# One stage instead of five between attention and the feed-forward network of a two-block layer kernel

## The reference

```
proj = rmsnorm(x, norm1_g) @ w_in           # x_rnn, g_rnn, q/k/v twice, f_logit, gates
x_rnn = causal_dwconv(x_rnn, 4 taps)
r, i  = sigmoid(x_rnn by blocks @ w_r + b_r), sigmoid(x_rnn by blocks @ w_i + b_i)
a     = exp(-8 * r * softplus(-a_param))
h_t   = a_t * h_(t-1) + sqrt(1 - a_t^2) * (i * x_rnn)_t      # the recurrence over 1024 steps
y_rnn = gelu(g_rnn) * h
y_diff, y_fox = two attentions              # 512 channels each
g = sigmoid(gates + gate_b)                 # three times 1024 channels
m = g0 * (y_rnn @ w_br_rnn) + g1 * (y_diff @ w_br_diff) + g2 * (y_fox @ w_br_fox)
x = x + m @ w_out
h = rmsnorm(x, norm2_g)                     # goes into the feed-forward network
```

## Time and profile before

| | |
|---|---|
| three runs | 3396.48, 3399.34, 3399.64 us |
| the profiled execution | 3396.45 us, its span in the trace 3394.7 us |
| PE busy in the span | 3130.7 us (92%) |
| DVE, ACT, POOL busy | 1425.9, 1123.5, 754.4 us |
| granted TensorE clock, mean | 0.953 of full speed |
| the five stages | about 664 to 1485 us of the span |

### The profile page before, as it was taken

One profiled execution on the slowest core, in us unless ns is written; L12 is line 12 of the kernel. 1 busy time (PEld: TensorE's weight loads), 2 busy tenths in 40 slices (PEclk: granted clock), 3 DMA queues, 4 the chain that ended last, 5 costly groups with the idle time before them and its releaser, 6 DMA issues. The chain is left out here.

```text
span 3394.7 us, 40123 instructions
## 1 busy us (share of the span) xinstructions
PE 3130.7 (92%) x15115; PEld 2555.2 (75%) x15115; DVE 1425.9 (42%) x2254; ACT 1123.5 (33%) x1466; POOL 754.4 (22%) x482
## 2 busy tenths in 40 slices
PE   8998899899989799979999999968799999999988
PEld 6776777678867587767888878847687888878766
DVE  4355133311135421143443343454434465555766
ACT  4344133321146521132322222232232445324332
POOL 2000100022211122111212211242423233123333
PEclk9999999999999899979999999979699999899979
DMA  3100210022221112232111111125031311222223
GB/s 127 49 23 7 63 32 29 10 59 65 62 49 42 46 56 74 87 51 72 48 39 43 58 47 37 31 87 93 10 87 47 100 38 32 100 45 69 75 81 118
DMA packets 275400, 194.00 MB, mean 57 GB/s; under 512 B 66504, under 2 KB 246856, under 8 KB 275280
## 3 DMA queue, kind: packets, MB, share of 16 engines
q1 hardware_dynamic: 273168, 191.33, 19.9%
q10 hardware_dynamic: 2112, 1.05, 0.1%
HBM read 165.77 MB, written 26.57 MB: 57 GB/s over the span
## 5 line engine op out<-in xcount | busy, mean ns | idle before, releaser
L136 POOL TENSOR_TENSOR w_low<-w_raw,w_high 128x1024 fp32r<-128x1024 f32 (+1 forms) x178 | 411.0, 2309 | 1846.6 <-ACT w_high L129 1842.2
L154 PE MATMUL pu<-act_high,w_high 128*128 128x512 f32 x704 | 276.5, 393 | 12.3 <-POOL w_low L136 8.6
L154 PE MATMUL pu<-act_low,w_high 128*128 128x512 f32 x704 | 276.1, 392 | 0.0
L154 PE MATMUL pu<-act_high,w_low 128*128 128x512 f32 x704 | 275.9, 392 | 0.0
L129 ACT ACTIVATE w_high<-w_raw 128x1024 fp32r<-128x1024 f32 (+1 forms) x178 | 177.2, 996 | 275.1 <-PE py L154 92.8
L154 PE MATMUL pg<-act_high,w_high 128*128 128x512 f32 x512 | 202.1, 395 | 28.6 <-ACTq L615 24.3
L154 PE MATMUL pg<-act_low,w_high 128*128 128x512 f32 x512 | 201.0, 393 | 0.0
L154 PE MATMUL pg<-act_high,w_low 128*128 128x512 f32 x512 | 200.5, 392 | 0.0
L639 DVE TENSOR_TENSOR gate<-gate,py 128x1024 f32<-128x1024 f32 x24 | 29.3, 1222 | 389.7 <-PE py L154 389.7
L154 PEld LDWEIGHTS pu<-act_high,w_high 128*128 128x128 f32 x704 | 133.5, 190 | 41.2 <-POOL w_low L136 9.3
L1631 DVE TENSOR_TENSOR x<-x,pd 128x512 f32<-128x512 f32 x176 | 118.1, 687 | 93.8 <-PE pd L1560 93.8
(11 more groups left out here) (640 smaller groups left out, 7509.8 us busy)
## 6 DMA issues: line engine op xcount, KB each, us to landing
w_raw<-in_w_in SPq DMA_DIRECT2D x106, 512.0 KB, 4.1
w_raw<-in_ffn_up SPq DMA_DIRECT2D x44, 512.0 KB, 3.8
w_raw<-in_w_out SPq DMA_DIRECT2D x24, 512.0 KB, 4.5
v_raw<-in_ffn_down SPq DMA_DIRECT2D x11, 1024.0 KB, 5.0
decay<-acum_rows SPq DMA_DIRECT2D x16, 512.0 KB, 3.7
x_ring<-in_x SPq DMA_DIRECT2D x8, 512.0 KB, 9.5
m_part<-gate SPq DMA_DIRECT2D x8, 512.0 KB, 3.0
w_raw<-in_w_br_rnn SPq DMA_DIRECT2D x8, 512.0 KB, 6.2
```

Source lines behind the costliest of these rows:

```text
L136: pool.tensor_tensor(self.low[slot][:, 0:nk, :], self.raw[slot][:, 0:nk, :], self.high[slot][:, 0:nk, :].bitcast(F32), ALU.subtract).then_ ...
L154: last = pe.matmul(out[:, h, :] if not halves else out[h], w[slot][:, k, :], x[:, k, cols], start=(n == 0), stop=(n == 3 * nk - 1))
```

## The change

The five stages become one, `stage_mix_branches`. In it:

- The two attended branches run as before. Their last turn loads and splits the recurrence's first tiles as ordinary tiles of the same two slots. `gate_b` is loaded for all three gates at the start (3 loads instead of 2), then the next tiles, then the eight small loads and the first `wr` and `wi`.
- The recurrence runs as before, its first turn written out with waits for the banks of the branches. Its PSUM pairs are those of the gates and outputs of the branches. Its SBUF buffers lie over M's place.
- The last branch is written out in 16 tiles in the order gate 0, gate 1, y 0, gate 2, y 1, ..., gate 7, y 6, y 7. In the recurrence's last turn ACT does the third split and gate 0's sigmoid before the last copy to `YH`. `other` has two buffers.
- Chunks 0 to 5 of M are split during the last two tiles, 6 and 7 as they come. M goes into `AH` and `AL` as before.
- X lies over `YH` and is loaded block by block in eight DMAs after the last use of `YH`. SP issues the third row tile's load behind them. The four row tiles of the second half of the columns are kept whole, high and low, over `YL`'s place.
- The first half of the columns goes as before, row tile by row tile over all blocks. The second half goes block by block: `rest(b)` is all 8 chunks for one block (24 matmuls), in four banks in turn. After each of them, the block before is transposed for the FFN. The squares, the root, the scaling and the splits of one block run beside the next block's matmuls.

```diff
-        stage_branches(core, [(1, w_diff, 4, 0), (2, w_fox, 4, 4)], columns(w_in, 0, D), part_out=core.m_part)
-        stage_rnn(core, [(0, gate(0)), (1, w_rnn[:, 0:P])])
-        stage_branches(core, [(0, w_rnn, KD, 0)], list(enumerate(rows_tiles(w_out, KD)[:2])), part_in=core.m_part)
+        X = nc.alloc_sbuf_tensor_at("x", [P, NB, D], F32, offset=core.yh_at)
+        stage_mix_branches(core, X, columns(io["ffn_up"][0], 0, D_FF))
     with ExitStack() as ctx:
-        X = sbuf(core, ctx, "x", [P, NB, D])
-        stage_rows(core, core.AH, core.AL, KD, w_out, X, whole=core.M, load_acc=io["x"][0])
-        stage_norm_to_channels(core, X, io["norm2_g"][0], ahead=columns(io["ffn_up"][0], 0, D_FF))
+        assert nc.sbuf_base == core.yh_at
+        sbuf(core, ctx, "x_place", [P, NB, D])
```

The order of the last branch, SP's program from the recurrence on, and what ACT does in the last turn and at the end:

```diff
+    order = [("gate", 0)]
+    for n in range(KD):
+        if n + 1 < KD:
+            order.append(("gate", n + 1))
+        order.append(("y", n))
...
+                for p in range(len(order)):
+                    load_last(p)
+                    if order[p][0] == "y" and order[p][1] + 1 < KD and order[p][1]:
+                        load_other(order[p][1] + 1)
+                for t in range(NG):
+                    load_rows(t)
+                    if t == 1:
+                        sp.wait_ge(W.s("used", 1), ROWS_AT + 1)
+                        for b in range(NB):
+                            sp.dma_start(X[:, b, :], io["x"][0][steps(b), :]).then_inc(sem(f"x_loaded{b}"), 16)
+                for t in range(NG, 2 * NG):
+                    load_rows(t)
...
+                    if not more:
+                        last_split(2)
+                        last_gate(0)
                     act.wait_ge(sem("y"), n + 1)
...
+                for p in range(1, len(order)):
+                    last_split(p + 2)
+                    what, n = order[p]
+                    if what == "gate":
+                        last_gate(n)
+                    if (what, n) == ("gate", KD - 1):
+                        for m in range(KD - 2):
+                            m_high(m)
+                    elif what == "y" and n >= KD - 2:
+                        m_high(n)
```

PE's part behind the last branch:

```diff
+                def rest(b):
+                    pe.wait_ge(sem("added"), b + 1)
+                    if b >= 4:
+                        pe.wait_ge(sem("whole"), b - 3)
+                    for kk in range(KD):
+                        r, k = kk // G, kk % G
+                        if b == 0 and k == 0:
+                            pe.wait_ge(sem("rest_low"), r + 1)
+                        for i, (x, v) in enumerate(((AH, RH), (AL, RH), (AH, RL))):
+                            last = pe.matmul(banks[:, b % 4, :], x[:, kk, steps(b)], v[r][:, k, :],
+                                             start=(kk == 0 and i == 0), stop=(kk == KD - 1 and i == 2))
+                    last.then_inc(sem("rest"), 1)
+
+                def turn_rows(b):
+                    pe.wait_ge(sem("scaled"), b + 1)
+                    pe.wait_ge(sem("added"), NB)
+                    if b >= 2:
+                        pe.wait_ge(sem("low"), b - 1)
+                    for k in range(KD):
+                        last = pe.transpose(turned[b % 2][:, k, :], scaled[b % 2][:, k * P:(k + 1) * P], ident[:, :])
+                    last.then_inc(sem("turned"), 1)
+
+                for b in range(NB):
+                    rest(b)
+                    if b:
+                        turn_rows(b - 1)
+                turn_rows(NB - 1)
```

More of the change, by code:

```diff
@@ new lines, in _ @@
+                for t in range(NG):
+                    slot, turn = row_place(t)
+                    WR.wait(pe, slot, turn)
+                    for b in range(NB):
+                        if t == 0 and b in (0, 2):
+                            pe.wait_ge(sem("last_gate"), KD - 1 + b // 2)
+                        elif t == 0 and b in (4, 6):
+                            pe.wait_ge(sem("weighed"), KD - 1 + (b - 4) // 2)
+                        for k in range(G):
+                            kk = t * G + k
+                            if b == 0:
+                                pe.wait_ge(sem("m_low"), kk + 1)
+                            for i, (x, v) in enumerate(((AH, WR.high), (AL, WR.high), (AH, WR.low))):
+                                last = pe.matmul(banks[:, b, :], x[:, kk, steps(b)], v[slot][:, k, :],
+                                                 start=(kk == 0 and i == 0), stop=(kk == KD - 1 and i == 2))
+                        if t == NG - 1:
+                            last.then_inc(sem("out"), 1)
+                    if t < NG - 1:
+                        last.then_inc(W.s("used", slot), 1)
@@ new lines, in m_low @@
+                def m_low(n):
+                    dve.wait_ge(sem("m_high"), n + 1)
+                    dve.tensor_tensor(AL[:, n, :], M[:, n, :], AH[:, n, :].bitcast(F32), ALU.subtract).then_inc(sem("m_low"), 1)
+                dve.wait_ge(sem("yl"), KD + 1)
+                for n in range(KD):
+                    slot, turn = place(at["y", n])
+                    if n == KD - 1:
+                        for m in range(KD - 2):
+                            m_low(m)
+                    dve.wait_ge(sem("last_gate"), n + 1)
+                    dve.wait_ge(W.s("used", slot), turn + 2)
+                    dve.tensor_tensor(gate[n % 2][:, :], gate[n % 2][:, :], flat2(pY[n % 2]), ALU.mult).then_inc(sem("weighed"), 1)
+                    dve.wait_ge(sem("weighed"), n + 1)
+                    dve.wait_ge(sem(f"other{n % 2}"), 16 * (n // 2 + 1))
+                    dve.tensor_tensor(M[:, n, :], gate[n % 2][:, :], other[n % 2][:, :], ALU.add).then_inc(sem("total"), 1)
@@ new lines, in _, with low @@
+                m_low(KD - 2)
+                m_low(KD - 1)
+                for b in range(NB):
+                    dve.wait_ge(sem(f"x_loaded{b}"), 16)
+                    dve.wait_ge(sem("out"), b + 1)
+                    dve.tensor_tensor(X[:, b, halves[0]], X[:, b, halves[0]], banks[:, b, :], ALU.add).then_inc(sem("added"), 1)
+                dve.wait_ge(sem("gain_loaded"), 16)
+                def low(b):
+                    dve.wait_ge(sem("high"), b + 1)
+                    dve.tensor_tensor(AL[:, :, steps(b)], turned[b % 2], AH[:, :, steps(b)].bitcast(F32), ALU.subtract).then_inc(sem("low"), 1)
@@ L735 @@
+                low(NB - 2)
+                low(NB - 1)
 BUCKETS, MAX_DIST = 32, 128
@@ L1686, in first_block @@
     gate = lambda g: w_in[:, GATES_AT + g * D:GATES_AT + g * D + P]
[L1687 removed]
+    w_diff = io["w_br_diff"][0]
     core.M = nc.alloc_sbuf_tensor_at("m_top", [P, KD, SEQ], F32, offset=nc.sbuf_top - 4 * KD * SEQ)
```

551 lines of the change are left out of this document (260 added, 291 removed).

## The result

The changed kernel took 3337.48 us (median of 4 runs, 3333.2 to 3339.15), beside 3397.91 us for the kernel before (4 runs). The ratio is 0.9821, with a 95% interval of 0.9804 to 0.9838. A second series gave 3334.05 us (5 runs) beside 3398.82, and a ratio of 0.9817, 0.9804 to 0.9830. The forecast was 3337.0. The span of the profiled execution went from 3394.7 to 3337.4 us.

A forecast was written before the change was run, and what follows sets the result against it. PE was taken to bound every stage, through its matmuls and waits. Savings of 11.9 + 20.7 + 9.9 + 19.1 less 0.4 give 61.2 us, so 3335.2 profiled; forecast 3337, range 3330 to 3352 (3331 to 3341: 80%).

The forecast's parts named there:

- Border 1: Attended branches to recurrence: a 9.40 us wait and 2.5 us of half clock go, saving 11.9 us.
- Border 2: Recurrence to last branch: an 18.97 us wait and 1.7 us of half clock go, saving 20.7 us.
- Border 3: Last branch to rows: an 8.21 us wait and 1.7 us of half clock go, saving 9.9 us.
- Border 4: Rows to norm and norm to FFN: 14.9 us instead of 34.0, saving 19.1 us.
- the third gate load: Opening of the stage: one more load issue ahead of the first sigmoid's release costs 0.4 us, possibly 0 to 0.6.
- The predicted slack of 4.6 at y0: Start of the last branch: y_low ready at about 1176.5, y0 starting at 1181.1, so PE does not wait.
- what POOL does to DVE: End of the last branch: the sum m_top takes 3.13 us instead of 1.2, ending with POOL's w_low.
- Rival B: A new wait inside the one stage, likeliest SP issuing X's loads slowly: 3355; with smaller slips 3342 to 3357, 14%.
- The tail: Behind rest(7): 4.1 us to scaled(7), 1.1 to 2.0 for its transposes, 3.6 to the stage's end; 9.2 us.
- Rival C: Rows, rest and turns at 1.2 GHz because of short waits for DVE: a loss of 23 us, 3422; 2%.
- the rule that was weighed: Cycling through PSUM banks idles PE enough for the clock to swing; rest and turn part would be at half clock.
- The signs that were named: Among others: inner-border waits gone, clock 1.00 from about 675 to the rest blocks' end, FFN's first matmul at about 1424.

The follow-up runs named there:

- second profiles: The changed kernel and the kernel before, each run and profiled once more with nothing edited: 3334.05 us and 3393.94 us.
- the first two experiments: Changed kernel with one old wait put back: px of channel 0 for the last partial sum's store, 3345.95 us; gate 0 for the last y_low, 3353.22 us.

## Why the prediction was right

From rows of both traces each term can be worked out as it was predicted; the start of px of channel 0 in the kernel before, without its wait, is 948.28 less 9.40 = 938.88.

| Term | before | after | saved | predicted |
|---|---|---|---|---|
| Border 1: px of channel 0 possible, to first pr | 938.88 to 972.56 = 33.68 | 939.59 to 961.36 = 21.77 | 11.9 | 11.9 |
| Border 2: first pr to end of the last branch | 972.56 to 1354.50 = 381.94 | 961.36 to 1322.25 = 360.89 | 21.05 | 20.7 |
| Border 3: rows and rest, without turns | 1354.50 to 1451.53 = 97.03 | 92.48 less six turns 5.46 = 87.02 | 10.0 | 9.9 |
| Border 4: turns, norm, stage's end | 34.04 | 5.46 + 9.99 = 15.45 | 18.6 | 19.1 |
| Sum | | | 61.6 | 61.6 |

(1354.50 is the printed end of the last branch; by the distance of two starts it is 1354.35, which moves 0.15 us from the second row to the third.) The 0.4267 us between starts at the 1.2 GHz level, for which the prediction names, does not stand there. The trace of the kernel before has it, for 10 matmuls behind the first border and 7 behind each of the next two.

Seen as a whole, the length fell by 62.0 (the first stage itself is 0.45 shorter), and the stage starts 1.16 later, of which 0.67 is the opening wait (5.32 to 5.99). For the third gate load 0.4 was taken, with a bound of 0.6. In the second profiles the opening wait is 5.79 before and 6.04 after, 0.25 apart, so the term lies between 0.25 and 0.67 and no run separates the load from this spread. The rest of the 1.16 comes from before the stage. So the feed-forward layer's first matmul came 60.85 us earlier, at 1424.72, "about 1424" having been said.

**Border 1.** px of channel 0 began at 939.59, and the store, the softplus and the taps were ready in time: xc ended at 959.03 + 1.28 = 960.31, PE needed it at 961.36. That is 1.05 us of slack where 1.6 was counted (ready at 958.9). Putting the wait back cost 11.1 us up to the last rest block. The step held, but this cover is the thinnest of all.

**Border 2.** The predicted slack of 4.6 at y0 was 4.8, and the experiment with the gates beside their branch used it up to within 0.1 us. The last branch took 1322.25 less 1147.75 = 174.50 us for 768 matmuls, 174.2 if warm from end to end. No cold start.

**Border 3.** Here the prediction stood on what POOL does to DVE. The timelines of POOL and of DVE around the end of the branch:

```profile
1312.77 2.40 POOL L136 TENSOR_TENSOR w_low<-w_raw,w_high 128x1024 fp32r<-128x1024 f32 x1 [8.38 <-ACT w_high L129]
...
1323.64 2.40 POOL L136 TENSOR_TENSOR w_low<-w_raw,w_high 128x1024 fp32r<-128x1024 f32 x1 [8.48 <-ACT w_high L129]
```

```profile
1312.89 3.35 DVE L785 TENSOR_TENSOR m_top<-gate,other 128x1024 f32<-128x1024 f32 x1
1316.16 6.89 DVE L772 TENSOR_TENSOR act_low<-m_top,act_high 128x1024 fp32r<-128x1024 f32 x6
1322.97 1.21 DVE L782 TENSOR_TENSOR gate<-gate,mix_banks 128x1024 f32<-128x1024 f32 x1
1324.22 2.91 DVE L785 TENSOR_TENSOR m_top<-gate,other 128x1024 f32<-128x1024 f32 x1
1327.05 2.43 DVE L772 TENSOR_TENSOR act_low<-m_top,act_high 128x1024 fp32r<-128x1024 f32 x2
```

The last low part ends at E + 7.2 (E being 1322.25), E + 7.6 was predicted. PE needs it at E + 32.7, since the three row tiles with chunks 0 to 5 come first, 48 matmuls or 10.9 us each. With the border put back all of it was a wait, of 7.06.

**Rival B**, the row tile that comes late behind X, did not happen. SP issued all eight loads of X in 3.93 us, 0.49 each, and not at the 3.2 each that the rival took from the opening:

```profile
1322.44 3.93 SPq L456 DMA_DIRECT2D x<-in_x  x8
```

The tile's split began at E + 14.4 (predicted 14.5), its low part ended at E + 17.9 (18.0), and the slack was 3.9 (3.8). Of the second half's four tiles the low parts ended at E + 28.1, 32.9, 35.4 and 40.3, where 28, 33, 36 and 41 had been said. The reason given against this rival was weaker than it looked. Of the 6 MB issued in the opening by 11.12 us, DMA had moved about 3 (263 GB/s over 11.12 us), so some 3 MB and not 6 were unfinished, and of the 6.49 us one issue took 5.02. In the experiment with the spare loads SP issued those eight, with the eight of X just ahead of them, in 5.17 us from 1326.74 on, 0.65 each, while 3 to 5 MB were unfinished. So a queue of that size did not bring the pace of 3.2; what held SP in the opening stays open. That experiment shows both sides of the slack: the slack is real, and it is small enough that 4 MB more on the same queue brings just that wait.

**Border 4.** Six turns were predicted at 0.95 us each and took 0.91: the first and the seventh transposes stand (1414.73 - 1376.65) / 6 = 6.35 apart, of which a rest block is 5.44. The tail was 9.99 instead of 9.2: 3.97 to the last scaled (predicted 4.1), 1.97 for the last transposes, which ran at half clock (1.1 to 2.0 had been said, and 1.5 is what the sum of 9.2 holds), and 4.05 to the stage's end (3.6). The tail is thus 0.8 longer, the six turns 0.2 shorter, which makes the 0.5 us by which this term was too large. Where the last transposes took 1.09 us, as in the first two experiments, the tail was 9.1.

**Rival C**, the clock. The stretch from row half 2 to the last rest block, in which DVE and PE share four banks in turn:

```profile
1366.00:1414.00 48.00, 48.00 (x237) 40.17 (x236) 21.32 (x27) 19.01 (x30) 4.76 (x2) 1.00 0.04 10
```

PE is busy for 48.00 of 48.00 us at a granted clock of 1.00. By the rule that was weighed (the Trainium skill, TensorE: Matmul & The Clock Gate, section on a second HAM failure mode; HAM is its name for the clock gate) the cycling through PSUM banks would have cost clock; the trace does not agree in this kernel. But the rule speaks of a PE that idles between the groups, and here it did not idle, so this stretch shows that going through banks in turn costs no clock by itself; it does not test what the idling would cost. The signs that were named came as well: the clock is 1.00 from 675 us to the end of the rest blocks (1414.7), and no wait of PE stands between 1366 and 1414.7.

**The one number not foreseen: 3.7 us given back in a place that the change does not touch.** The feed-forward layer began 60.85 us earlier, yet the span fell by 57.3. I followed PE's starts through both traces. At the first transposes of the second block nearly all of it was still there, 60.5 us (2255.61 to 2195.09); for the mixing of its third part it was 56.8 (2329.39 to 2272.62). Rows of the changed kernel, first as profiled after the change, then of the same kernel once more:

```profile
2195.09 1.97 PE L3465 MATMUL turned<-ident,scaled 128*128 128x128 f32 x8 [12.28 <-DVE scaled L3578]
...
2217.45 0.76 PE L3481 MATMUL pu<-act_high,w_high 128*128 128x512 f32 x1 [1.98 <-DVE act_low L3583]
...
2250.73 0.50 PE L3481 MATMUL pu<-act_high,w_high 128*128 128x512 f32 x1 [1.13 <-POOL w_low L136]
2272.62 0.39 PE L3481 MATMUL turned<-act_high,w_high 128*128 128x512 f32 x1
```

```profile
2192.88 1.97 PE L3465 MATMUL turned<-ident,scaled 128*128 128x128 f32 x8 [12.23 <-DVE scaled L3578]
...
2215.24 0.77 PE L3481 MATMUL pu<-act_high,w_high 128*128 128x512 f32 x1 [1.98 <-DVE act_low L3583]
...
2244.68 0.50 PE L3481 MATMUL pu<-act_high,w_high 128*128 128x512 f32 x1 [0.43 <-POOL w_low L136]
2266.57 0.39 PE L3481 MATMUL turned<-act_high,w_high 128*128 128x512 f32 x1
```

The 24 matmuls from `pu` to the next transposes take 8.44 us in the one and 6.91 in the other. In the table by stretches these are

```profile
2217.40:2225.90 8.50, 8.45 (x25) 6.65 (x26) 3.85 (x5) 1.45 (x3) 0.00 (x0) 0.64 0.44 177
2236.80:2250.70 13.90, 12.80 (x48) 10.09 (x48) 13.69 (x7) 3.04 (x4) 4.42 (x1) 0.88 0.01 1
```

```profile
2215.20:2222.15 6.95, 6.91 (x24) 5.59 (x25) 3.85 (x5) 1.45 (x3) 0.00 (x0) 0.79 0.54 219
2233.05:2244.68 11.63, 11.19 (x49) 8.94 (x49) 11.46 (x6) 2.37 (x3) 3.73 (x1) 1.00 0.01 1
```

In the longer case PE stays at the 1.2 GHz level for more matmuls behind the same wait of 1.98 us (1.5 us more), and falls back to it for a while at the second place, at a clock of 0.88 instead of 1.00 (1.6 us more). The wait behind that is 1.13 us instead of 0.43. The instructions are the same and so are the waits up to there. The stretch took 73.2 to 73.9 us in nine of the thirteen traces of this study and 77.5 in four; the same program has had both, so it is not tied to the change. In the nine, 6 to 8 matmuls behind that wait ran at the 1.2 GHz level, in the four 13 or 14. Its rival (a length set by the instruction times of each kernel) falls. The profiled executions of the changed kernel also fit: 3339.15 us with the long stretch, 3333.7 with the short one. Whether the spread of the runs that left no trace comes from this place is likely but not shown. What decides between the two lengths stays open.

For the forecast this means that 3337.0 against 3337.48 is closer than the working deserves. The working gave 61.2 us of span, thus 3333.5; the second trace of the changed kernel, with the short stretch as in the trace of before, has 3332.0. With the short stretch on both sides the spans fell by 62.7 (3394.7 to 3332.0) or, with the second profile of the kernel before, by 60.2 (3392.2 to 3332.0), around the 61.2 of the working. The mechanism and the size were right; that the forecast came within 0.5 us was luck. I had added 1.8 us because the runs' median lay above the profiled execution, and that margin happens to lie inside this spread.

## What to carry to other kernels

Where one engine is over 90% busy, look at the borders between stages rather than at the share: the four here cost 10 to 21 us each in the kernel before, and they added up. Put back one at a time, the first three were 7 to 16 us of waiting and 1.6 to 3.1 of half clock behind it. A border can be priced ahead to a few tenths of a us if one lists, for each first instruction behind it, when its last input is ready and when the engine could be there. The same list names the thin covers (here 1.05 us at the first convolution, 3.9 at row tile 2, 4.8 at y0) that the next edit must not use up, and the waits left inside the loops, which gave the next 7 to 10 us.

A profile of one execution can hold a few us in a place that has nothing to do with the change. Compare starts at several points along the span before a cause is looked for, and run the unchanged kernel twice when the missing part lies far behind the edit.

## What the runs showed of the hardware that I had not expected

The half-clock start behind a short wait has no fixed length. Behind the same 1.98 us wait 6 matmuls ran at the 1.2 GHz level in one execution of a program and 14 in another, and a second start followed only in the latter; 3.8 us of 3334 in all. Behind the same 2.93 us wait eight transposes took 1.09 us in some kernels and 1.97 in others. A length that contains such a place can hide or add 1 us.

A DVE operation with two inputs in SBUF does not just slow down beside POOL, it ends a fixed time after POOL has ended. The sum m_top, 1.2 us of work, took 3.13 us, 3.35 and 2.91. In all three cases, as in the other six sums of the last branch, it ends 1.1 us behind the end of the POOL operation that had started before it: 1206.90 against 1205.82, 1316.24 against 1315.17, 1327.13 against 1326.04. The Trainium skill (SBUF — State Buffer, section on the two separate sides) calls the port pair that both use an exclusive lock, held for a whole instruction. The three rows agree. The later DVE starts within such a POOL operation, the less it costs. With one input in a PSUM bank nothing is lost: in the feed-forward layer of the changed kernel a step of its convolution that reads `pu` ran for its 1.28 us from 1455.54, wholly within a POOL operation from 1455.21 to 1457.59, and the product of two SBUF inputs behind it ran from 1456.93 to 1458.67, again 1.1 us behind POOL's end.
